# A two-layer decoder trunk: the first norm's modulation in quarters, summed by VectorE and TensorE together, tokens in four loads, rotary angles last

## Chip, cores and metric

One core of one Trainium2 chip. The metric is the device time of one execution in microseconds (us), taken as the median of several runs. A profile is one further execution, recorded by the hardware profiler. Engines: TensorE (PE; PEld is its weight load), VectorE (DVE), ScalarE (ACT), GpSimd (POOL) and SyncE (SP, which here only issues DMAs).

## What is computed

A two-layer causal decoder trunk over 512 tokens of 1024 features, conditioned by a vector c. Each sublayer is a root-mean-square norm with a learned gain, a modulation by c, a mixer or a gated convolutional FFN, a norm, a gate and a residual add. Only the opening matters here: the modulation of the first norm, the normed input h, the values of the first mixer, and the rotary tables that its queries and keys need.

```python
def rms_norm(x, g, eps=1e-6):
    return x * lax.rsqrt(jnp.mean(x * x, axis=-1, keepdims=True) + eps) * g

def ada_mod(c_act, w, b, n):
    return jnp.split((c_act @ w + b)[:, None, :], n, axis=-1)

c_act = jax.nn.silu(c)
ang = positions[..., None] * inv            # rope tables: cos(ang), sin(ang)
shift, scale, gate = ada_mod(c_act, mod_mix_w[0], mod_mix_b[0], 3)
h = rms_norm(x, norm_pre_mix[0]) * (1.0 + scale) + shift
y = dilated_mixer(h, a_w_qkv[0], a_w_o[0], cos, sin)   # 3 groups of 8 heads: q and k rotated, v plain
```

## The kernel before

Each engine has its own program, and semaphores tie them together. A signal such as lo_ready counts the events of a stream; `wait_ge(*at.done(sig, n))` waits for the n-th event from the present count. The order of work on an engine is written out by hand.

**Products.** Values are f32, split into a head (whi, hhi) and a rest (wlo, hlo); a product is three matmuls. Weights come in chunks of 512 KB into raw (three slots). ScalarE makes the head (`split_head`, L1341), VectorE the rest (`split_rest`, L1871, which raises lo_ready), and TensorE waits for lo_ready of the chunk that it multiplies. Chunks 0 to 3 are the values of group 0, chunk 4 is the first of load_pair(0), the first pair of heads.

**The opening, TensorE.** It turns rows of vectors into columns (`turn_rows`, L758; L766 for the rotary constants), then waits for the scaled x (xn0) and turns it, 8 tiles of features by 4 of tokens (L839), into four banks of PSUM, from which ScalarE copies z0 (L1504). Warm-up matmuls (`keep_warm`, L609, 512 columns of bf16, result unused), then `start_sums(0)`: the shift and scale of the first four tiles of features, as 8 sums over partitions of macc0 (L637, each a matmul with one column of f32, two records in the trace). Warm-ups again, then the value products of group 0 (`values_chunk(0, c)`, L800 and L816), 24 matmuls of 512 columns per chunk. Between chunks 0 and 1 stands `shift_columns(4)`: one eighth of the modulation's weights multiplied straight from mstart with csil, 16 matmuls of one column (L781, 32 records). Inside chunk 1 stands start_sums(1), before chunk 2 eight warm-ups. Behind chunk 3 comes first_pair: for each of six chunks a projection of 24 products (L583 to L585), starting with chunk 4.

**The modulation.** csil is silu(c), a column per tile of 128 rows. mod_mix_w for shift and scale is loaded into mstart in eight loads of 1 MB, j = 0 to 7 (L515), rows of 512 columns (2 KB). VectorE multiplies and adds row tiles into macc0 in chains of 8 (`start_chain`, L2162 and L2164: 512 columns each), TensorE sums them over partitions, VectorE adds the bias (`sums_read`, L2183 to L2186) and raises m_known; ScalarE and VectorE then make h: hhi (L1514), tmp (L1513 or L2196), hlo (L2198), which raises h_ready. Work is in halves: four tiles of features at a time.

**x.** SP loads c, five norm vectors, then x in one load of 2 MB (L488), then mstart and the value chunks in turn. ScalarE issues the small loads of its own queue, waits for x, squares four token tiles (L1492), GpSimd takes the root (L2600, L2603) once for the four, ScalarE and VectorE scale two tiles each (L1498, L2151).

**The angles.** VectorE computes them (L2123 to L2133) as soon as the vectors are there, ahead of the scaling and of all sums. ScalarE makes the sine and cosine tables (L1536) before its values_chunk(0, 0). VectorE's last steps of the opening are: split_rest of chunk 3, wait for the sines, the two table products (L2221, L2222), then split_rest of chunks 4, 5 and 6 with halves of the later modulation between them (L2059, L2063), then the rotations (L2233 to L2238). ScalarE's are: the copies of the values (L1521), split_head of chunk 6, the masks (L1548, L1550).

GpSimd makes the masks (L2575) first, then the root, then fetches the later modulations (L2630) once the last load of mstart has landed.

Of the kernel before, what the change touches and what calls it, by code (L numbers as in the profile page):

```python
# [29 lines left out]
P = 128  # L30
# [84 lines left out]
def yoco_trunk(nc, x, c, positions, mod_mix_w, mod_mix_b, mod_ffn_w, mod_ffn_b,  # L115
# [16 lines left out]
    WARM, WARM_START, WARM_SUMS = 12, 8, 12  # L132
# [10 lines left out]
    with ExitStack() as ctx:  # L143
# [234 lines left out]
        x_landed = signal("x_landed", "x_landed", 1, 16)  # L378
# [20 lines left out]
        x_scaled_too = signal("x_scaled_too", "x_scaled_too")  # L399
# [8 lines left out]
        VECS, TABLES, ROWS = 6, 7, 6  # L408
# [55 lines left out]
        def _(sp):  # L464
# [20 lines left out]
            for dst, src in ((PRE_MIX, norm_pre_mix), (POST_MIX, norm_post_mix), (PRE_FFN, norm_pre_ffn), (POST_FFN, norm_post_ffn)):  # L485
                sp.dma_start(rows[dst:dst + 2 * DT, 0, :], src.rearrange("l (r n) -> (l r) n", n=P)).then_inc(*at.here(vec_landed))
            sp.dma_start(rows[KVN:KVN + DT, 0, :], kv_norm.rearrange("(r n) -> r n", n=P)).then_inc(*at.here(vec_landed))
            sp.dma_start(x_tok[:], x[0].rearrange("(t p) d -> p t d", p=P)).then_inc(*at.here(x_landed))  # L488
# [23 lines left out]
            for half in range(2):  # L512
                for j in range(4 * half, 4 * half + 4):
                    col, k0 = half * 4 * P + (D if j % 4 > 1 else 0), j % 2 * (D // 2)
                    sp.dma_start(mstart[:, j], mod_mix_w[0][k0:k0 + D // 2, col:col + 4 * P].rearrange("(k p) n -> p k n", p=P)).then_inc(mods_landed[j].sems[0], 16)  # L515
                for n in (2 * half, 2 * half + 1):
                    load_values(0, n)
# [59 lines left out]
        def _(pe):  # L577
# [9 lines left out]
            def project(rhs, k0, k1, ksteps=DT, first=True, last=True, stride=P, col0=0, done=True, open_=True):  # L587
# [187 lines left out]
            def shift_columns(j):  # L775

                bank = job()
                pe.wait_ge(*at.done(mods_landed[j]))
                for n in range(4):
                    for k in range(DT // 2):  # L780
                        ins = pe.matmul(bank[:, n:n + 1], mstart[:, j, k, tile_cols(n)], csil[:, k:k + 1],  # L781
                                        start=(k == 0), stop=(k == DT // 2 - 1))
                job_done(ins)

            def start_sums(half):

                pe.wait_ge(*at.done(m0_summed, 2 * half + 1))
                columns_of([macc0[:, n, :] for n in range(8)])

            def values_chunk(g, c, between=None):  # L790
# [3 lines left out]
                if g == 0 and c in (0, 2):  # L794
                    for k in (2 * c, 2 * c + 1):
                        pe.wait_ge(*at.done(h_ready, k))
                        w = slice(k % 2 * value_cols(g), (k % 2 + 1) * value_cols(g))
                        for t in range(NT):
                            for n, (a, b) in enumerate(((hhi, whi), (hhi, wlo), (hlo, whi))):
                                mm = pe.matmul(ps[:, t, 0:value_cols(g)], a[:, k, tile_cols(t)], b[:, slot, w], start=(k == 0 and n == 0), stop=False)  # L800
                    mm.then_inc(*at.here(chunk_used))
                    at.passed("chunk")
                    return
                if g == 0:
                    pe.wait_ge(*at.done(h_ready, 2 * c + 1))
                for t in range(NT):
                    if t == 2 and between is not None:
                        between()
                    if g and c == 0:
# [21 lines left out]
            pe.wait_ge(*at.done(x_scaled, 1))  # L831
            pe.wait_ge(*at.done(x_scaled_too, 1))
            for k in range(DT):
                if k < 4:
                    pe.wait_ge(*at.done(t_free, -1 - k % 2))
                else:
                    pe.wait_ge(*at.done(z_out, k - 4))
                for t in range(NT):
                    ins = pe.transpose(ps[:, 4 + k % 4, tile_cols(t)], xn0[:, t, tile_cols(k)], identf[:])  # L839
                ins.then_inc(*at.here(xn_turned, k))  # L840
            pe.wait_ge(*at.done(masks_ready))
            keep_warm(WARM_SUMS, ps[:, 3, :])
            pe.wait_ge(*at.done(z_out, DT - 1))
            start_sums(0)
            keep_warm(WARM_SUMS, ps[:, 3, :])
            values_chunk(0, 0)
            shift_columns(4)
            values_chunk(0, 1, lambda: start_sums(1))
            keep_warm(WARM_START, ps[:, 4, :])
            values_chunk(0, 2)  # L850
            values_chunk(0, 3)
# [471 lines left out]
        def _(act):  # L1323
# [147 lines left out]

            for j, v in enumerate((b_lambda_q1, b_lambda_q2, b_lambda_k1, b_lambda_k2)):
# [1227 lines left out]
```

## Times and profile before

| | us |
|---|---|
| median of 3 runs | 1405.76 (1404.61 to 1405.80) |
| the profiled execution, its own time | 1405.17 |
| its span in the profile | 1403.4 |
| TensorE busy | 1353.8 (96%) |
| VectorE busy | 918.2 (65%) |
| ScalarE busy | 582.2 (41%) |
| GpSimd busy | 147.4 (11%) |
| granted TensorE clock, mean | 0.991 of full |

A busy share is over the whole span. All of the change lies in the first 70 us of it, so the rows below are of that stretch. Times in them count from the span's start.

### The profile page before, as it was taken

To read this page: it belongs to the slowest core of one execution; us is meant where nothing else is said; L and a number is where in the kernel's file an instruction comes from. 1 tells how busy PE (TensorE), PEld (TensorE's weight loads), DVE (VectorE), ACT (ScalarE), POOL (GpSimd) and SP (SyncE) were. 2 spreads that over 40 slices of the span, in tenths; PEclk is the share of its full clock that TensorE was granted. 3 is DMA by queue.
4 is the path that set the end of the run, shared out by engine and by line. 5 is a ranking of instruction groups with operands and counts; after the bars stand their busy time and mean duration, and the time that the engine had idled before them with its cause. 6 is when DMAs were issued, how large, how long until landed. Compare 5 with 4: busy or idle time off the path is not lost.

```text
span 1403.4 us, 17895 instructions
## 1 busy us (share of the span) xinstructions
PE 1353.8 (96%) x6936; PEld 1106.9 (79%) x6936; DVE 918.2 (65%) x1618; ACT 582.2 (41%) x994; POOL 147.4 (11%) x238
## 2 busy tenths in 40 slices
PE   4999999999899999999999999998999999999998
PEld 3789788888788788887887777776888778887886
DVE  7687889886678777764556648997567444443223
ACT  4543344446543334332115537777543333332112
POOL 2001001000411111100113001221220000000000
PEclk9999999999999999999999999999999999999999
DMA  9437424331256555553661232112145333333331
GB/s 332 157 90 221 143 91 151 106 106 46 71 158 207 166 178 181 181 165 101 201 193 65 71 90 61 52 55 91 31 145 161 99 90 91 90 96 99 90 102 64
DMA packets 168665, 171.47 MB, mean 122 GB/s; under 512 B 5269, under 2 KB 140806, under 8 KB 168582
## 3 DMA queue, kind: packets, MB, share of 16 engines
q1 hardware_dynamic: 154224, 119.59, 28.2%
q0 software_dynamic: 13824, 50.34, 10.7%
q8 instruction: 55, 0.90, 0.3%
q10 hardware_dynamic: 534, 0.41, 0.1%
q14 instruction: 28, 0.23, 0.0%
HBM read 168.22 MB, written 2.10 MB: 121 GB/s over the span
## 4 chain that ended last, share of the span: by engine, by line
PE 80%; DVE 9%; ACT 5%; issue 2%; POOL 2%; DMA 1%; SPq 0%; POOLq 0%; ACTq 0%; DVEq 0%
PE ps L655 20%; PE ps L583 15%; PE ps L585 15%; PE ps L584 15%; PE ps L1109 2%; PE ps L816 2%; PE ps L906 2%; ACT prob L1761 2%; PE ps L894 2%; PE ps L626 1%; PE ps L1238 1%; PE ps L637 1%; DVE wlo L1871 1%; DVE prob L2488 1%; POOL osum L2667 1%
## 5 line engine op out<-in xcount | busy, mean ns | idle before, releaser
L583 PE MATMUL ps<-hhi,whi 128*128 128x512 f32 (+1 forms) x1008 | 396.1, 393 | 2.7 <-DVE hlo L1958 2.1
L1871 DVE TENSOR_TENSOR wlo<-raw,whi 128x1024 fp32r<-128x1024 f32 x200 | 244.1, 1221 | 233.8 <-ACT whi L1341 233.7
L585 PE MATMUL ps<-hhi,wlo 128*128 128x512 f32 (+1 forms) x1008 | 387.2, 384 | 0.0
L584 PE MATMUL ps<-hlo,whi 128*128 128x512 f32 (+1 forms) x1008 | 387.1, 384 | 0.0
L1341 ACT ACTIVATE whi<-raw 128x1024 fp32r<-128x1024 f32 x200 | 209.8, 1051 | 244.5 <-PE ps L655 169.5
L583 PEld LDWEIGHTS ps<-hhi,whi 128*128 128x128 f32 x1008 | 189.5, 188 | 45.2 <-DVE hlo L1958 2.9
L585 PEld LDWEIGHTS ps<-hhi,wlo 128*128 128x128 f32 x1008 | 189.4, 188 | 41.4
L584 PEld LDWEIGHTS ps<-hlo,whi 128*128 128x128 f32 x1008 | 189.6, 188 | 39.0 <-issue 1.0
L2063 DVE SCALAR_TENSOR_TENSOR macc<-mraw,csil,macc 128x256 f32<-128x256 f32 x294 | 142.4, 484 | 13.2 <-DMA mraw<-in_mod_ffn_w_dram 4.0
L655 PE MATMUL ps<-whi,ghi 128*128 128x512 f32 x352 | 110.1, 394 | 1.7 <-DVE tmp L2427 1.7
L655 PE MATMUL ps<-whi,glo 128*128 128x512 f32 x352 | 109.1, 391 | 0.0
L655 PE MATMUL ps<-wlo,ghi 128*128 128x512 f32 x352 | 108.9, 390 | 0.0
L2411 DVE SCALAR_TENSOR_TENSOR tmp<-ps,convc,tmp 128x511 f32<-128x511 f32 x88 | 65.9, 748 | 47.8 <-ACT tmp L1699 46.3
L1709 ACT ACTIVATE ghi<-tmp 128x512 fp32r<-128x512 f32 x44 | 27.8, 632 | 154.3 <-DVE tmp L2427 154.3
L1699 ACT ACTIVATE tmp<-ps,convc 128x512 f32<-128x512 f32 x44 | 34.2, 778 | 109.1 <-PE ps L585 109.1
L655 PEld LDWEIGHTS ps<-whi,ghi 128*128 128x128 f32 x352 | 65.7, 188 | 16.8 <-DVE tmp L2427 2.5
L655 PEld LDWEIGHTS ps<-wlo,ghi 128*128 128x128 f32 x352 | 66.1, 188 | 15.1
L655 PEld LDWEIGHTS ps<-whi,glo 128*128 128x128 f32 x352 | 66.1, 188 | 14.1
L2630 POOL DMA_DIRECT2D mraw<-in_mod_ffn_w_dram x48 | 36.4, 759 | 333.3 <-DVE macc L2063 259.3
L2427 DVE TENSOR_TENSOR tmp<-ps,tmp 128x512 f32<-128x512 f32 x44 | 30.4, 690 | 57.3 <-issue 45.0
L2600 POOL TENSOR_SCALAR stat<-stat 128x1 f32<-128x1 f32 (+1 forms) x27 | 14.7, 545 | 431.5 <-ACT tmp L1387 419.0
L1706 ACT ACTIVATE tmp<-tmp 128x512 f32<-128x512 f32 x44 | 27.9, 633 | 52.0 <-DVE tmp L2411 52.0
(306 smaller groups left out, 1961.1 us busy)
## 6 DMA issues: line engine op xcount, KB each, us to landing
mraw<-in_mod_ffn_w_dram POOLq DMA_DIRECT2D x48, 512.0 KB, 4.5
raw<-in_ffn_w_gate_dram SPq DMA_DIRECT2D x44, 512.0 KB, 3.7
raw<-in_ffn_w_up_dram SPq DMA_DIRECT2D x44, 512.0 KB, 3.7
raw<-in_ffn_w_down_dram SPq DMA_DIRECT2D x44, 512.0 KB, 3.6
mraw<-in_mod_mix_w_dram POOLq DMA_DIRECT2D x32, 512.0 KB, 3.9
raw<-in_a_w_qkv_dram SPq DMA_DIRECT2D x28, 512.0 KB, 4.6
mstart<-in_mod_mix_w_dram SPq DMA_DIRECT2D x8, 1024.0 KB, 14.6
mraw<-in_kv_mod_w_dram POOLq DMA_DIRECT2D x16, 512.0 KB, 3.9
```

The costliest lines, as they stand in the source:

```text
L583: pe.matmul(out_, whi[:, slot, cols], rhs_hi, start=first, stop=False)
L584: pe.matmul(out_, whi[:, slot, cols], rhs_lo, start=False, stop=False)
L585: return pe.matmul(out_, wlo[:, slot, cols], rhs_hi, start=False, stop=last)
L655: mm = pe.matmul(ps[:, 2 * t + half, :], part[:, k, tile_cols(t)], w[:, half * 512:half * 512 + 512], start=(first and n == 0), stop=(last ...
L816: mm = pe.matmul(ps[:, t, 0:value_cols(g)], a[:, k, tile_cols(t)], b[:, slot, w], start=(k == 0 and n == 0), stop=(k == DT - 1 and n == 2))
L1341: act.activation(whi[:, slot, :], raw[:, slot, :], ACT.Copy).then_inc(*at.here(hi_ready, ahead))
L1699: act.activation(tmp[:, 0, :], acc[at.at("bank", 3)], ACT.Identity, bias=convc[:, base + 3 * FT + ft:base + 3 * FT + ft + 1], scale=convc[ ...
L1871: dve.tensor_tensor(wlo[:, slot, :], raw[:, slot, :], head, ALU.subtract).then_inc(*at.here(lo_ready, ahead))
L2063: ins = dve.scalar_tensor_tensor(sum_, src, factor, sum_, ALU.mult, ALU.add)
L2411: ins = dve.scalar_tensor_tensor(conv, bank[:, 0:T - shift], tap(t, ft), conv, ALU.mult, ALU.add)
L2427: dve.tensor_tensor(tmp[:, 2, :], bank, tmp[:, 1, :], ALU.mult).then_inc(*at.here(acc_free))
L2630: pool.dma_start(mraw[:, at.at("mod", 2)], src).then_inc(*at.here(m_landed))
```

## The change

- The tokens x are loaded in four loads, a signal each, right behind c on SP's queue; the norm vectors move to ScalarE's queue, the bias and convolution tables to GpSimd's. ScalarE squares a token tile as it lands, GpSimd takes each root by itself, VectorE scales all four.
- The modulation is taken in quarters of two tiles of features: 16 loads of 512 KB, rows of 256 columns (1 KB). Of the eight row tiles of a quarter VectorE adds five in a chain (`chain_sums`), TensorE multiplies the other three straight from mstart (`sums_of`) and adds VectorE's sum into the same columns of PSUM (`close_sums`).
- Value products go a tile of features at a time (`first_values`), with the next quarter's sums between the two tiles of a chunk. The warm-ups have 384 columns (`keep_ready`): 20 ahead of the transposes, 20 ahead of the values, 4 behind each of the first three chunks.
- positions are loaded behind the last quarter of mstart, the angles computed behind the last tile of h, the sines made behind ScalarE's last value chunk. GpSimd's masks come behind its roots.

The diff, cut:

```diff
-    WARM, WARM_START, WARM_SUMS = 12, 8, 12
+    WARM, WARM_FIRST, WARM_QUARTER = 12, 20, 4
...
+        QUARTERS, Z_BANKS = 4, (4, 7, 2, 3, 4, 7, 2, 3)
+        SUMS_V, SUMS_P = ((0, 1, 2), (0, 1)), ((3,), (2, 3))
...
-            sp.dma_start(x_tok[:], x[0].rearrange("(t p) d -> p t d", p=P)).then_inc(*at.here(x_landed))
+            for t in range(NT):
+                sp.dma_start(x_tok[:, t, :], x[0][t * P:(t + 1) * P, :]).then_inc(x_landed.sems[t], 16)
...
+            for q in range(QUARTERS):
+                for j in (2 * q, 2 * q + 1):
+                    rows_of = mod_mix_w[0][j % 2 * (D // 2):(j % 2 + 1) * (D // 2), :]
+                    for part, col in enumerate((2 * q * P, D + 2 * q * P)):
+                        sp.dma_start(mstart[:, j, :, part * 2 * P:(part + 1) * 2 * P],
+                                     rows_of[:, col:col + 2 * P].rearrange("(k p) n -> p k n", p=P)).then_inc(mods_landed[j].sems[0], 16)
+                if q == QUARTERS - 1:
+                    sp.dma_start(posi[:], positions.to_broadcast([P, T])).then_inc(*at.here(pos_landed))
+                load_values(0, q)
...
+            def keep_ready(n, bank):
+
+                for _ in range(n):
+                    pe.matmul(bank[:, 0:3 * P], identb[:], causal[:, 0:3 * P], start=True, stop=True)
...
+            def sums_of(q, half):
+
+                if half == 0:
+                    job()
+                bank = turned[at.at("tjob", 2)]
+                pe.wait_ge(*at.done(mods_landed[2 * q + half], 1))
+                for k in SUMS_P[half]:
+                    for n in range(4):
+                        pe.matmul(bank[:, n:n + 1], mstart[:, 2 * q + half, k, tile_cols(n)], csil[:, 4 * half + k:4 * half + k + 1],
+                                  start=(half == 0 and n == 0 and k == SUMS_P[0][0]), stop=False, skip_group_check=True)
+
+            def close_sums(q):
+
+                bank = turned[at.at("tjob", 2)]
+                pe.wait_ge(*at.done(m0_summed, q))
                 for n in range(4):
+                    ins = pe.matmul(bank[:, n:n + 1], macc0[:, 4 * (q % 2) + n, :], onesf[:, 0:1], start=False, stop=True, skip_group_check=True)
                 job_done(ins)
...
+            def first_values(c):
...
+                for k in (2 * c, 2 * c + 1):
+                    pe.wait_ge(*at.done(h_ready, k))
+                    w = slice(k % 2 * value_cols(0), (k % 2 + 1) * value_cols(0))
+                    for t in range(NT):
+                        for n, (a, b) in enumerate(((hhi, whi), (hhi, wlo), (hlo, whi))):
+                            mm = pe.matmul(ps[:, t, 0:value_cols(0)], a[:, k, tile_cols(t)], b[:, slot, w], start=(k == 0 and n == 0), stop=(k == DT - 1 and n == 2))
...
+                        if c < QUARTERS - 1 and (k % 2, t) == (0, NT - 1):
+                            sums_of(c + 1, 0)
+                            sums_of(c + 1, 1)
+                        if c < QUARTERS - 1 and (k % 2, t) == (1, 0):
+                            close_sums(c + 1)
...
+                else:
+                    keep_ready(WARM_QUARTER, ps[:, 4, :])
...
+            keep_ready(WARM_FIRST, ps[:, 3, :])
+            pe.wait_ge(*at.done(c_ready))
+            pe.wait_ge(*at.done(x_scaled, NT - 1))
...
+            for k in range(4):
+                turn_x0(k)
+            sums_of(0, 0)
+            for k in range(4, DT):
+                turn_x0(k)
+            sums_of(0, 1)
+            close_sums(0)
+            keep_ready(WARM_FIRST, ps[:, 0, :])
+            pe.wait_ge(*at.done(z_out, DT - 1))
+            for c in range(DT // 2):
+                first_values(c)
             pe.wait_ge(*at.done(masks_ready))
...
+            act.preload_act_table(ACT.Exp)
...
+            split_head(0)
             h_head(0, False)
             h_head(1, True)
             split_head(1)
-            h_head(2, True)
+            h_head(2, False)
             h_head(3, True)
             split_head(2)
+            h_head(4, False)
+            h_head(5, True)
+            values_chunk(0, 0)
+            h_head(6, False)
+            h_head(7, True)
+            for c in range(1, DT // 2):
+                values_chunk(0, c)
             act.wait_ge(*at.done(angles_ready))
             for dst, j in ((sinT, 0), (cosT, 1)):
                 act.activation(classed(dst[:]), by_class(ang[:, j, :]), ACT.Sin).then_inc(*at.here(sines_ready))
                 at.passed("sines_ready")
-            values_chunk(0, 0)
-            for k in range(4, DT):
-                h_head(k, False)
-            for c in range(1, DT // 2):
-                values_chunk(0, c)
...
+            scale_tokens(0)
+            scale_tokens(1)
             bank = job_ready()
             job_read(dve.tensor_copy(small[:, NEGLAM:NEGLAM + 1], bank[:, 0:1]))
+            scale_tokens(2)
             for dst, n in ((bcol[:], NMOD), (convc[:, 0:CONV], CONV), (convc[:, CONV:2 * CONV], CONV)):
                 read_columns(dst, n)
+            scale_tokens(3)
...
+            chain_sums(0)
+            sums_read(0)
             split_rest(0)
             h_rest(0, False)
             h_rest(1, True)
+            for q in range(1, QUARTERS):
+                chain_sums(q)
+                if q < QUARTERS - 1:
+                    split_rest(q)
+                else:
+                    at.passed("chunk")
+                    split_rest()
+                sums_read(q)
+                h_rest(2 * q, False)
+                h_rest(2 * q + 1, True)
+            angles()
             at.passed("h", DT)
 
             dve.wait_ge(*at.done(sines_ready, 1))
...
-            pool.wait_ge(*at.done(x_squared, NT - 1))
-            rms(X_RMS, X_SUM, slice(0, NT)).then_inc(*at.here(x_scale))
+            for t in range(NT):
+                pool.wait_ge(*at.done(x_squared, t))
+                rms(X_RMS, X_SUM, slice(t, t + 1)).then_inc(*at.here(x_scale, t))
...
-            pool.wait_ge(*at.done(mods_landed[DT - 1]))
+            pool.wait_ge(*at.done(mods_landed[DT - 1], 1))
```

## Rows read from the trace of the kernel before

**Rows 1.** The chain of waits, 0 to 110 us: start, us, what.
```profile
21.50 6.33 PE ps L839 x32
...
37.68 5.49 PE ps L800 x24
43.17 3.46 PE ps L781 x32
46.63 4.45 PE ps L816 x12
51.09 1.68 PE ps L637 x16
52.77 2.88 PE ps L816 x12
...
62.88 5.49 PE ps L816 x24
```

**Rows 2.** Timeline, VectorE from 40 us: start, us, engine, line, operation.
```profile
59.48 0.48 DVE L2221 TENSOR_SCALAR sinT<-sinT,small 128x512 f32<-128x512 f32 x1
...
60.58 1.23 DVE L1871 TENSOR_TENSOR wlo<-raw,whi 128x1024 fp32r<-128x1024 f32 x1
```

**Rows 3.** Timeline, the start of the opening, 0 to 20 us.
```profile
6.41 0.39 DVE L2095 TENSOR_TENSOR lamr<-lamr 1x128 f32<-1x128 f32 x1 [1.11 <-DMA posi<-in_positions_dram]
...
12.43 1.06 ACT L1492 ACTIVATE tmp<-x_tok 128x1024 f32<-128x1024 f32 x1 [4.27 <-DMA x_tok<-in_x_dram]
...
18.11 1.05 POOL L2603 TENSOR_TENSOR stat<-stat,neghalf 128x4 f32<-128x4 f32 x1
```

**Rows 4.** The page: a group of GpSimd's DMA issues, then issues with us to landing.
```profile
L2630 POOL DMA_DIRECT2D mraw<-in_mod_ffn_w_dram x48 | 36.4, 759 | 333.3 <-DVE macc L2063 259.3
...
mraw<-in_mod_mix_w_dram POOLq DMA_DIRECT2D x32, 512.0 KB, 3.9
...
mstart<-in_mod_mix_w_dram SPq DMA_DIRECT2D x8, 1024.0 KB, 14.6
```

**Rows 5.** Windows: us, busy of five engines, PEclk, DMA share, GB/s.
```profile
20.00:30.00 10.00, 8.50 (x43) 7.24 (x44) 9.61 (x15) 6.74 (x11) 0.00 (x0) 1.00 1.05 387
48.00:49.00 1.00, 1.00 (x4) 0.77 (x3) 1.00 (x2) 0.00 (x0) 0.00 (x0) 0.50 0.00 0
51.00:52.00 1.00, 1.00 (x12) 1.00 (x10) 0.00 (x0) 0.00 (x0) 0.00 (x0) 1.00 1.10 326
```

**Rows 6.** Timeline: the last eight transposes of x, and ScalarE's copies.
```profile
26.68 1.16 PE L839 MATMUL ps<-identf,xn 128*128 128x128 f32 x8
...
26.66 2.05 ACT L1504 ACTIVATE z<-ps 128x512 f32<-128x512 f32 x4
```

**Rows 7.** Timeline: a chain of sums, and the first two tiles of h.
```profile
25.89 5.48 DVE L2164 SCALAR_TENSOR_TENSOR macc<-mstart,csil,macc 128x512 f32<-128x512 f32 x7
...
33.88 0.81 ACT L1514 ACTIVATE hhi<-z,modc,presc 128x512 fp32r<-128x512 f32 x1 [5.17 <-DVE presc L2186]
...
36.14 0.69 DVE L2198 TENSOR_TENSOR hlo<-tmp,hhi 128x512 fp32r<-128x512 f32 x1 [0.65 <-ACT hhi L1514]
```

**Rows 8.** Timeline: the first and the last of VectorE's steps of the angles.
```profile
10.27 0.43 DVE L2123 CAST ang<-posi 128x512 f32<-128x512 int32 x1
...
16.00 0.69 DVE L2133 TENSOR_SCALAR ang<-ang 128x1024 f32<-128x1024 f32 x1
```

**Rows 9.** Timeline, ScalarE: the last copy of values, and the head of chunk 6.
```profile
68.41 0.60 ACT L1521 ACTIVATE vA<-ps 128x512 f32<-128x512 f32 x1 [0.78 <-PE ps L816]
68.91 1.05 ACT L1341 ACTIVATE whi<-raw 128x1024 fp32r<-128x1024 f32 x1
```

**Rows 10.** Timeline, ScalarE: the sine table's load and the two tables.
```profile
40.85 1.28 ACT L1536 ACT_TABLE_LOAD   x1
42.14 1.15 ACT L1536 ACTIVATE sinT<-ang 128x512 f32<-128x512 f32 x1
...
43.20 1.13 ACT L1536 ACTIVATE cosT<-ang 128x512 f32<-128x512 f32 x1
```

More of the change, by code:

```diff
@@ L783, in shift_columns @@
                 job_done(ins)
[L785 to L790, printed above, removed]
+            def first_values(c):
+                slot = at.at("chunk", 3)
+                pe.wait_ge(*at.done(lo_ready))
+                for k in (2 * c, 2 * c + 1):
[4 more added lines that the diff above has]
+                            mm = pe.matmul(ps[:, t, 0:value_cols(0)], a[:, k, tile_cols(t)], b[:, slot, w], start=(k == 0 and n == 0), stop=(k == DT - 1 and n == 2))
+                        if k == DT - 1 and t < NT - 1:
+                            mm.then_inc(*at.here(v_ready))
+                            at.passed("vtok")
+                        if c < QUARTERS - 1 and (k % 2, t) == (0, NT - 1):
[3 more added lines that the diff above has]
+                            close_sums(c + 1)
+                mm.then_inc(*at.here(chunk_used))
+                at.passed("chunk")
+                if c == DT // 2 - 1:
+                    at.passed("vout", NT)
+                else:
+                    keep_ready(WARM_QUARTER, ps[:, 4, :])
@@ L792, in values_chunk @@
+            def values_chunk(g, c):
                 pe.wait_ge(*at.done(lo_ready))
                 slot = at.at("chunk", 3)
[L794 to L803, printed above, removed]
@@ L804, in values_chunk @@
-                if g == 0:
-                    pe.wait_ge(*at.done(h_ready, 2 * c + 1))
                 for t in range(NT):
-                    if t == 2 and between is not None:
-                        between()
-                    if g and c == 0:
+                    if c == 0:
                         pe.wait_ge(*at.done(v_out, t - NT))
@@ L2101, in _ @@
             read_columns(vcol[:], NVEC)
-            read_columns(small[:, 0:5], 5)
             dve.wait_ge(*at.done(c_exped))
@@ L2162, in start_chain, with chain_sums @@
+            def chain_sums(q):
+                sum_ = macc0[:, 4 * (q % 2):4 * (q % 2) + 4, :].rearrange("p a n -> p (a n)")
+                for half in range(2):
+                    dve.wait_ge(*at.done(mods_landed[2 * q + half], 1))
+                    for k in SUMS_V[half]:
+                        src, row = mstart[:, 2 * q + half, k, :], 4 * half + k
+                        if half == 0 and k == 0:
                             ins = dve.tensor_scalar(sum_, src, csil[:, row:row + 1], None, ALU.mult)
@@ L2192, in h_rest @@
                     gain, shift = presc[:, k:k + 1], modc[:, MIX[0] + k:MIX[0] + k + 1]
[L2193 removed]
+                    dve.wait_ge(*at.done(m_known, k // 2))
                     if k >= 3:
@@ L2580, in _ @@
             chain(pool.memset(neghalf[:], -0.5))
+            chain(pool.memset(causal[:], 0.0))
             chain(pool.memset(identf[:], 0.0))
```

189 lines of the change are left out of this document (63 added, 126 removed).

## The prediction

> **What bounds the kernel now.** The chain of waits over the first 110 us [rows 1] says what sets the end of each stage. TensorE is on it nearly throughout and, from 68.4 us on, without a hole; over the span it is 96% busy. So the change, which touches only the code before the projections of the first pair of heads, is worth what it does to one instant: when TensorE can start that pair. Before, that is 68.37 us: the last value product ends there [rows 1], and the next matmul follows at once.
>
> Behind the transposes of x (from 21.50 us) come warm-up matmuls, 8 column sums, warm-ups again, and at 37.68 us the value products. From there to 68.37 us are 30.7 us: 96 products at 22.0 us (24 in 5.49), and 8.7 us of others: the 16 sums of shift_columns (3.46), 12 products at nearly half pace (4.45 instead of 2.75), the 8 sums of start_sums (1.68), and eight warm-ups. Note the counts: 16 sums in the code are x32 in the row, 8 are x16. A sum of one f32 column goes in two passes and costs 3.46/16 = 0.216 us, nearly a product of 512 columns.
>
> The first pair needs weight chunk 4 split by VectorE, and in the code that split stands behind the sine and cosine tables. Before, VectorE makes the tables at 59.48 and splits chunk 4 at 60.58 us, ready at 61.8 [rows 2]: a cover of 6.5 us, because the angles were computed at 10 to 17 us and the sines in the middle of the value products.
>
> **The start.** The five norm loads now stand on ScalarE's queue ahead of five small ones, so the last small one is issued at about 4.3 us instead of 2.4. The last one before was consumed at 6.41 us, 4.0 after its issue [rows 3]; I take 8.0 now. VectorE waits for it before it reads the vectors, so the squares of x start at about 9.3 us instead of 12.43 [rows 3]; x, issued 2.2 us earlier, is no longer the late one. Four squares at a pitch of 1.18 end at 14.1; GpSimd's power took 1.05 for four columns [rows 3], for one column and its addition I take 1.0; VectorE's scaling of the last tile 0.75: 15.9 us. The seven table loads move to GpSimd's queue. A load of 512 KB occupies it 0.76 us [rows 4], so seven end by about 8 us, before its first root at 10.5, and land before VectorE reads them at 14.7: nothing; up to 2 us if they land late.
>
> TensorE does not go straight on: 20 warm-ups of 384 columns stand ahead of its wait for the scaled x, and can't start before the table rows are turned, about 15.4 us. What they cost depends on the clock. The windows give it as 1.00 [rows 5]. But of the 32 transposes, 6.33 us in all [rows 1], the last eight take 1.16 [rows 6], so the 24 before them take 5.2, a pitch of 0.215, half the pace: TensorE was at its lower level (1.2 GHz) for 5.2 us after its idle time. At 0.32 us each until then and 0.17 after, 20 warm-ups cost 5.8 us; at full clock 3.4. The Trainium skill, in "TensorE: Matmul & The Clock Gate", Part 1, says the half-rate state is the default of an idle array; by that rule the trace agrees, in its transposes and not in its recorded clock. By the recorded clock alone all that follows would come 2.4 us earlier; I go by the pace of the transposes. They now start at 21.2 us: nothing gained on 21.50 so far.
>
> They are at full clock then, so ScalarE's copies (a pitch of 0.49 [rows 6]) and the 12 sums between and behind them set the pace: 1.7 for 16 transposes, 0.9 for four sums, 1.7 again, 1.7 for eight sums, 0.9 for the closing four: 7.0. Then 20 warm-ups of 0.17: the value products start 10.4 us after the transposes, at **31.6 us** instead of 37.7. Beside these warm-ups VectorE reads the sums, splits chunk 0 and makes the first two tiles of h.
>
> **The quarters.** TensorE, per quarter: 24 products 5.49, 16 sums 3.46, four warm-ups 0.69: 9.6 us. VectorE: five chained sums instead of eight, 0.5 + 4 x 0.78 = 3.6 (seven took 5.48 [rows 7]), a split 1.1, reading sums 0.5, two tiles of h 2.9 (33.88 to 36.8 [rows 7]): 8.1 us, beside TensorE. So TensorE bounds, and what VectorE gives up is paid by it at 0.216 a sum. Four times 5.49, three times 3.46 and 0.69 are 34.4 us, where there were 30.7. The value products would end at **66.0 us**.
>
> The clock comes on top. 12 sums in a row, three products, 4 sums: that is 3.46 us of sums in 4.15. Behind 3.46 us of sums in a row the windows show 0.50 [rows 5] and 12 products lost 1.7 us; behind 1.68 us of them 12 products took 2.88, hardly more than at full clock [rows 1]. The new stretch is nearer to the first. I take two drops in three quarters, 3.3 us; ends 0 and 6.6 (three, and one ahead of the values). End at **69.3 us**.
>
> Data are in time. The first stage moves 387 GB/s in rows of 2 KB and more; rows of 1 KB are now loaded, and a window with only these shows 326 [rows 5]. At that rate the last quarter lands at about 40 us and is wanted at 51. It turns late below some 240 GB/s.
>
> **The wait that is new.** The angles now stand behind the last tile of h on VectorE, at about 65 us, and the tables and the split of chunk 4 still stand behind them. The angles took 10.27 to 16.69 us, 6.4 us [rows 8]: done at 71. ScalarE first copies out the last values and splits the head of chunk 6, as at 68.41 and 68.91 before [rows 9]: free 1.7 us behind the last product, 71.0; then it loads the sine table (1.28) and makes the two (2.2) [rows 10]: 74.5. VectorE's table products take 1.1, the split of chunk 4 1.2 [rows 2]: ready at 76.9 us. TensorE, which went from values to pair without a pause, now idles 7.6 us behind the last product, whenever that comes. 76.9 - 68.3 = **+8.6 us**.
>
> Then it restarts on the lower level. Time at half pace loses half of itself: 2.6 us by the 5.2 after the idle time at the start, 1.7 by the drop behind the sums. The restart is the nearer row: +2.6. Ends 0 (the clock stays up) and 3.4 (twice the drop).
>
> Behind that nothing is new: VectorE has chunk 5, two mod halves and chunk 6 ahead of the first rotation, 6.2 us of work for a first chunk of 5.6 to 8.2; the masks on ScalarE fit there too. GpSimd's later modulations wait for the last quarter, 40 instead of 37.9 us, and aren't wanted before 65.
>
> **Sum:** start -6.1, longer value stage +3.7, drops +3.3 (0 to 6.6), 7.6 idle, restart +2.6 (0 to 3.4): +11.1 us. The profiled execution took 1405.17 us (span 1403.4), the median of the runs is 1405.76, 0.6 above. So 1416.3 in its terms, and **1416.9** as a median. A measurement of this kernel tells about 0.2%, 2.8 us, from no change.
>
> **Rivals.**
> A, slower, but less: the sums don't drop the clock, since they come in two parts with products between: +7.8, 1413.6.
> B, slower, and more: each quarter drops it, and so do the sums ahead of the values: +14.4, 1420.
> C, not slower: the tables don't hold the split, or come early enough, so that the pair starts behind the last product: without the idle time and its restart, +0.9 with two drops, -2.4 with none, and -4.8 with the opening warm-ups at full clock too: 1401 to 1406.7. It decides where the sines are done before about 64 us. Against: VectorE's text has the angles behind h_ready of the last tile, and before, the split at 60.58 did follow the tables. For: nothing but that the cover was large.
> D, much slower: loads late. Each 1 MB load is now two of 512 KB. Loads of 1 MB landed 14.6 us after issue [rows 4] while the queue moved 387 GB/s, so they overlap. Were the small ones not to, at 3.9 us each (a 512 KB load by itself [rows 4]), the 23 up to the last quarter would end at 90 us where 51 will do: +39 more, 1456. The Trainium skill, "DMA: Bandwidth & Descriptors", Bandwidth, asks for loads of 1 MiB or more; by its fit a load of 512 KB takes an estimated 3.2 us, which one after the other would give nearly the same.
>
> **Chances.** The forecast 0.48, A 0.18, B 0.14, all slower; C 0.11, of it 0.05 faster and 0.06 within 2.8 us; D 0.03, slower; an opening that comes out 3 us earlier, together with A and a cheap restart, 0.06, half of it within. So slower 0.86, same 0.09, faster 0.05. The range leaves out D and most of C: 1408.5 (A with an early opening or a restart at nothing) to 1421.5 (B, tables a little late).
>
> **What would show it.** Right: squares from 9 to 10 us; value products from 30 to 33 us and ending at 65 to 71; sums x24 and x8 a quarter; granted clock 0.50 in places inside the value products; angles on VectorE from 60 to 66; then a hole of TensorE of 7 to 8 us, ended by VectorE's split, and a first pair that starts at half level. Wrong: no such hole, or one under 5 us; sums at half the price; VectorE idle ahead of its sums on a DMA; or a first pair that starts below 72 us.

## The result, and the profile after

| | before | after |
|---|---|---|
| median, us (4 runs each, side by side) | 1405.78 (1404.61 to 1408.53) | 1424.70 (1420.18 to 1429.21) |
| ratio of times, 95% interval | 1 | 1.0135 (1.0114 to 1.0156) |
| profiled execution, its span, us | 1405.17, 1403.4 | 1429.21, 1427.4 |
| granted TensorE clock, mean | 0.991 | 0.983 |

Slower by 18.9 us in medians; 11.1 had been forecast, and the time lies above the range. The profiled execution of after is the slowest of its four: its span is 24.0 us longer. So the accounting below adds up to 24.0, and what was the same in every run is sorted out afterwards.

The chain of waits of after, 0 to 110 us; columns as in [rows 1]. L812 is a value product, L792 the sums straight from mstart, L800 the closing sums, L613 the warm-ups, L864 the transposes.

```profile
4.58 5.47 DMA row<-in_b_subln_dram
...
17.72 6.15 PE ps L613 x20
23.87 1.75 PE ps L864 x16
...
31.09 4.62 PE ps L613 x20
35.71 2.76 PE ps L812 x12
38.47 2.91 PE ps L792 x24
41.38 1.49 PE ps L812 x3
42.87 1.50 PE ps L800 x8
44.37 3.63 PE ps L812 x9
...
51.43 2.57 PE ps L792 x24
...
56.70 4.05 PE ps L812 x9
...
69.05 4.05 PE ps L812 x9
...
74.40 5.71 PE ps L812 x24
80.63 1.05 ACT whi L1368
81.70 1.28 ACT L1561
82.99 1.11 ACT sinT L1561
84.10 1.00 ACT cosT L1561
85.13 0.50 DVE sinT L2233
85.65 0.56 DVE cosT L2234
86.23 1.24 DVE wlo L1891
```

What to see. The value products start at 35.71 us; before, at 37.68 [rows 1]. The last ends at 80.11 (74.40 + 5.71); before, at 68.37. Each of the first three quarters has its sums, x24 and x8, with three products between them (1.49, 1.20 and 0.81 us) and nine behind them in 3.6 to 4.05 us. At full clock, where 24 take 5.49 [rows 1], three take 0.69 and nine 2.06. The last quarter, which has no sums in it, takes 5.71 for its 24. Then TensorE leaves the chain: ScalarE's head of chunk 6, the sine table's load, the two tables, VectorE's two table products and its split of chunk 4, in just the order of the prediction.

Windows of after: the first two while the first sums run, one in the nine products behind them, one in the hole, one in the first pair; columns as in [rows 5].

```profile
39.00:40.00 1.00, 1.00 (x11) 1.00 (x11) 0.21 (x1) 0.00 (x0) 0.11 (x1) 1.00 0.35 130
40.00:41.00 1.00, 1.00 (x9) 1.00 (x9) 0.00 (x0) 0.00 (x0) 1.00 (x2) 0.78 0.60 184
46.00:47.00 1.00, 1.00 (x4) 0.72 (x3) 0.47 (x1) 1.00 (x3) 0.00 (x0) 0.50 0.01 4
85.00:86.00 1.00, 0.00 (x0) 0.00 (x0) 0.84 (x2) 1.00 (x4) 0.00 (x0) 0.50 0.00 0
88.00:89.00 1.00, 1.00 (x3) 0.73 (x3) 0.96 (x3) 0.98 (x3) 0.00 (x0) 0.50 0.19 57
```

By windows of 0.5 us, the granted clock of after was at its lower level (1.2 GHz, 0.50 of full) from 30.3 to 33.7, 40.6 to 47.4, 54.2 to 61.0, 67.9 to 74.7 and 84.9 to 91.8 us: once for 3.4 us, ahead of the values, and four times for 6.8.

Timeline of after: the first and two later products of the first pair, with the idle time ahead of the first in brackets.

```profile
87.60 0.77 PE L587 MATMUL ps<-hhi,whi 128*128 128x512 f32 x1 [7.50 <-DVE wlo L1891]
...
91.58 0.48 PE L587 MATMUL ps<-hhi,whi 128*128 128x512 f32 x1
92.36 0.40 PE L587 MATMUL ps<-hhi,whi 128*128 128x512 f32 x1
```

A record of 0.39 or 0.40 is the full pace here (the step from one product to the next is 0.233 us, a third of 0.70). The first nine of the pair took 3.98 us (87.60 to 91.58) and not 2.10, so the restart cost 1.9 to 2.0.

| part of the 24.0 us | forecast | in this profile |
|---|---|---|
| value products start | -6.1 | -2.0 |
| value stage without a drop, 34.4 for 30.7 | +3.7 | +3.7 |
| drops of the clock in it | +3.3 | +10.0 (44.4 less 34.4) |
| TensorE idle | +7.6 | +7.5 |
| restart | +2.6 | +2.0 |
| later than the first pair | 0 | +2.8 |

The last row is not of the change. A load of the later modulation landed 7.1 us after its issue, the sums waiting for it came 27.4 us behind their reference point and not 25.9, and one stage of 48 products ran at a granted clock of 0.70 to 0.73 in 10.0 us and not 8.4. In the profiles of before and of all the experiments below, the same places showed 25.9 to 26.3 and 8.44 to 8.46. The part behind the start of the first pair differs from profile to profile anyway: 1335.0 us in before, 1339.8 in after, and 1333.2 (3) to 1340.0 (6) in the experiments. Without this row the profile's change is 21.2, and the medians' 18.9 lies 2 us under that; that the number of drops differs from run to run (shown below) would do for such a spread, but no run ties the one to the other.

### The profile page after: what moved, and what is told of

Read it like the earlier page. It is cut to its first block, busy times and chain, and to the rows that moved or that the text cites. A ratio compares the mean times of both kernels' runs of the same rounds, so it can differ in the third digit from the quotient of the medians.

```text
span 1427.4 us, 18078 instructions
## 1 busy us (share of the span) xinstructions
PE 1372.1 (96%) x7018; PEld 1122.1 (79%) x7020; DVE 914.5 (64%) x1616; ACT 580.6 (41%) x993; POOL 156.4 (11%) x251
## 4 chain that ended last, share of the span: by engine, by line
PE 80%; DVE 9%; ACT 5%; issue 2%; POOL 2%; DMA 1%; ACTq 0%; POOLq 0%; DVEq 0%
PE ps L664 19%; PE ps L587 15%; PE ps L589 14%; PE ps L588 14%; PE ps L1136 2%; PE ps L812 2%; PE ps L933 2%; ACT prob L1781 2%; PE ps L921 2%; PE ps L840 2%; PE ps L635 1%; DVE wlo L1891 1%; PE ps L1265 1%; DVE prob L2500 1%; PE ps L613 1%
## 5 line engine op out<-in xcount | busy, mean ns | idle before, releaser
L2439 DVE TENSOR_TENSOR tmp<-ps,tmp 128x512 f32<-128x512 f32 x44 | 30.3, 689 | 57.6 <-issue 45.2
L2607 POOL TENSOR_SCALAR stat<-stat 128x1 f32<-128x1 f32 x30 | 17.0, 566 | 438.8 <-ACT tmp L1414 420.3
```

What stands on the lines that cost most here:

```text
L2439: dve.tensor_tensor(tmp[:, 2, :], bank, tmp[:, 1, :], ALU.mult).then_inc(*at.here(acc_free))
```

## The experiments

Two theories of where the time is lost, and they don't exclude each other: **the tables** (the late angles hold the split of chunk 4, so TensorE idles and restarts low, 9 to 11 us) and **the row of sums** (12 one-column sums in a row let the clock drop, so each of three quarters loses over 3 us). The rival of the second: the sums cost what they cost by their number, or by what VectorE does, and not by their place. Medians of before below are those of the runs beside the experiment. The ratios are taken over all runs of a kernel and are not quite the quotient of the medians. The span of a single profile strays by some us from the medians, so verdicts go by ratios and by the times of the stages.

**1. Angles early.** After, with positions loaded on ScalarE's queue, the angles behind the first chain of sums, the sines behind split_head(2).

```diff
+            act.dma_start(posi[:], positions.to_broadcast([P, T])).then_inc(*at.here(pos_landed))
...
             chain_sums(0)
+            angles()
             sums_read(0)
...
             split_head(2)
+            act.wait_ge(*at.done(angles_ready))
+            for dst, j in ((sinT, 0), (cosT, 1)):
+                act.activation(classed(dst[:]), by_class(ang[:, j, :]), ACT.Sin).then_inc(*at.here(sines_ready))
```

> The changed kernel with the angles computed by VectorE behind its first chain of sums, where it sat idle for 8 us, and the sines made ahead of the fifth tile of h. Theory (the wait for the tables costs 7.5 us of idle TensorE and about 2 us of restart at half level): no hole in front of the first pair, the pair starts 7 to 9 us earlier at full clock, and the time falls by 9 to 11 us, to 1413.5 to 1415.5. Rival 1 (the split of chunk 4 is held by something else, or ScalarE's sines in the middle delay h by as much): a hole of over 4 us stays or moves into the value products, 1420 or more. Rival 2 (the later stage, where sums of the next modulation come late, absorbs it): the pair starts earlier, but the end moves by less than 5 us.

Measured: 1412.78 beside 1404.79, ratio 1.0057 (1.0034 to 1.0079); after itself has 1.0135. Its timeline, the last value product and the first of the pair:

```profile
76.08 0.40 PE L810 MATMUL ps<-whi,hlo 128*128 128x512 f32 x1
76.32 0.39 PE L585 MATMUL ps<-hhi,whi 128*128 128x512 f32 x1
```

No hole and no restart: 0.24 us apart, at full pace. The gain is 0.0078 of 1405, 11 us. The value stage still takes 42.6 us (33.70 to 76.3), with the drops in it (two windows, and from the chain the nine products of the quarter between them):

```profile
40.00:50.00 10.00, 10.00 (x39) 7.79 (x39) 6.85 (x12) 6.62 (x7) 1.62 (x2) 0.67 0.49 159
...
60.00:70.00 10.00, 10.00 (x49) 8.41 (x48) 4.62 (x10) 3.17 (x4) 0.00 (x0) 0.69 0.18 53
```

```profile
53.60 3.76 PE ps L810 x9
```

The sums stand as in after, and yet the three drops were not alike: by windows of 0.5 us the clock was at 0.50 for 6.8, 3.4 and 6.8 us. In the middle quarter it cost 1.7 us (3.76 for 2.06), the price of the drop in before.

**2. Late angles alone.** Before, with the same two moves made in it and nothing else.

```diff
             for c in range(1, DT // 2):
                 values_chunk(0, c)
+            act.wait_ge(*at.done(angles_ready))
+            for dst, j in ((sinT, 0), (cosT, 1)):
+                act.activation(classed(dst[:]), by_class(ang[:, j, :]), ACT.Sin).then_inc(*at.here(sines_ready))
...
             split_rest()
+            a0, a1, k0 = ang[:, 0, :], ang[:, 1, :], ang[:, 2, :]
...
             at.passed("h", DT)
```

> The kernel before, in which only the angles are moved behind the last tile of h and the sines behind the last values; loads, halves and sums stay as they were. Theory: a hole of 7 to 8 us ahead of the first pair and a restart at half level for 3 to 5 us: 8.5 to 10.5 us slower than before, 1414 to 1416.5. Rival (the cover of 6.5 us in the kernel before was real and the hole comes from the quarters): 0 to 2 us slower, 1405.5 to 1408.

Measured: 1416.61 beside 1404.79, ratio 1.0079 (1.0056 to 1.0102). The waits of TensorE (total, times, longest), then the chain:

```profile
PE ps L583 <- DVE wlo L1871: 7.5, 1, 7.5
```

```profile
60.30 5.51 PE ps L816 x24
66.33 1.05 ACT whi L1341
67.39 1.28 ACT L1541
...
71.93 1.24 DVE wlo L1871
```

The same hole of 7.5 us without anything else of the change. The chain shows why it has nothing to do with when the values end: it begins with ScalarE's work behind the last product (66.33) and runs 7 us from there. In this kernel the values end 2.6 us earlier, and the pair gains none of it. Of the 2.6, VectorE's being rid of the angles ahead of the scaling gave 0.9 (the 8 sums start at 30.58 us, not 31.46); the other 1.7 is that the clock did not drop ahead of the values in this profile (the 12 warm-ups there took 2.61 us, in before 4.30). Behind the hole the clock stayed at 0.50 until 78.2 us, so that the restart cost 2.4 us here.

**3. Sums spread.** After, with three sums behind each group of three products, and the closing sums one group later.

```diff
-                        if c < QUARTERS - 1 and (k % 2, t) == (0, NT - 1):
-                            sums_of(c + 1, 0)
-                            sums_of(c + 1, 1)
-                        if c < QUARTERS - 1 and (k % 2, t) == (1, 0):
+                        if c < QUARTERS - 1 and k % 2 == 0:
+                            piece_of(c + 1, t)
+                        if c < QUARTERS - 1 and (k % 2, t) == (1, 1):
                             close_sums(c + 1)
```

> The changed kernel with the same 12 sums per quarter put three behind each group of three products instead of 12 in a row. Theory (it is their crowding that drops the clock): the clock stays at 1.00, the value products take 35 to 37 us, time 7 to 10 us less, 1415 to 1418. Rival (their number sets the price; spread, each also breaks the products' pipeline): value stage of 42 us or more and 1423 to 1426, clock at 0.50 in the products or not.

Measured: 1415.40 beside 1404.79, ratio 1.0078 (1.0052 to 1.0105). A window of the value stage, then from the timeline the first of the pair:

```profile
40.00:50.00 10.00, 9.91 (x61) 8.18 (x60) 6.86 (x12) 3.18 (x4) 1.07 (x2) 1.00 0.44 144
```

```profile
76.40 0.77 PE L587 MATMUL ps<-hhi,whi 128*128 128x512 f32 x1 [7.51 <-DVE wlo L1901]
```

As many sums as in after, but the clock is at 1.00 throughout the values and the stage takes 35.9 us (33.0 to 68.9), not 44.4. The place of the sums was the cost, not their number. The hole stays at 7.51.

**4. VectorE takes all eight rows.** After, with only the four closing sums left on TensorE (three rows fewer for it, three more for VectorE).

```diff
-        SUMS_V, SUMS_P = ((0, 1, 2), (0, 1)), ((3,), (2, 3))
+        SUMS_V = ((0, 1, 2, 3), (0, 1, 2, 3))
...
-                            sums_of(c + 1, 0)
-                            sums_of(c + 1, 1)
```

> The changed kernel with all eight row tiles of a quarter summed by VectorE; TensorE only closes (4 sums a quarter instead of 16). Theory (TensorE's 12 one-column sums cost 2.6 us a quarter and drop its clock for 6.8 us each time): the granted clock stays at 1.00 through the value products, VectorE bounds with 10.5 us a quarter, the value products take 37 to 39 us instead of 44.4, and the stage ahead of them is 2 us shorter: 8 to 10 us less, 1415 to 1417. Rival (VectorE's three extra steps per quarter, 2.3 us, take back what TensorE gains; the drops come from the closing sums or the waits): value stage of 43 us or more, 1421 to 1425.

Measured: 1416.35 beside 1404.79, ratio 1.0077 (1.0052 to 1.0101). The waits of TensorE, the chain, a window:

```profile
PE ps L789 <- DVE macc L2172: 6.1, 3, 2.8
```

```profile
58.34 1.41 PE ps L789 x8
59.75 4.05 PE ps L801 x9
```

```profile
60.00:70.00 10.00, 10.00 (x34) 7.40 (x34) 8.10 (x16) 5.24 (x7) 0.00 (x0) 0.72 0.19 55
```

The value stage takes 40.2 us, because TensorE now waits 6.1 us for VectorE's sums. The time came out as expected (1415 to 1417), but neither the clock (1.00 throughout) nor the stage (37 to 39 us) did: behind four closing sums that had waited up to 2.8 us the clock dropped in all three quarters, twice for 3.4 us and once for 6.8, where nine products took 4.05 us again. So a row of 12 sums is one way to a drop, and a wait with a short row of sums behind it looks to be another; the two parts of that were not tried apart.

**5. Two rows of six.** As 3, but six sums behind the second group of the tile and six behind the fourth, closing behind the sixth group.

```diff
-                for half, k, n in pieces[3 * i:3 * i + 3]:
+                for half, k, n in pieces[6 * i:6 * i + 6]:
...
-                        if c < QUARTERS - 1 and k % 2 == 0:
-                            piece_of(c + 1, t)
+                        if c < QUARTERS - 1 and k % 2 == 0 and t % 2:
+                            piece_of(c + 1, t // 2)
```

> The changed kernel with the 12 sums of a quarter in two rows of six, behind the second and the fourth group of three products, the closing four behind the sixth group. It asks how crowded sums may stand. Theory (a row nearer to the 1.68 us of the kernel before, which kept the clock, does no harm; a row here is 1.3): clock at 1.00 in all three quarters, value stage 35 to 36.5 us, time as a_sums_spread, 7 to 10 us under the changed kernel. Rival (any row of sums beside another loses the clock in part of the quarters): value stage 38 to 42 us, 1418 to 1422.

Measured: 1416.47 beside 1406.62, ratio 1.0072 (1.0048 to 1.0097). A window of its value stage:

```profile
43.00:53.00 10.00, 9.92 (x60) 8.32 (x60) 6.80 (x12) 3.07 (x5) 0.00 (x0) 1.00 0.35 111
```

Clock 1.00 and a stage of 35.8 us. Rows of six sums (1.23 us in the chain) did no harm here with six products between them; rows of 2.6 to 2.9 us did in after.

**6. Closing sums late.** After with its row of 12, the closing four moved two groups of products back. The theory was that a drop lasted 6.8 us because a second row follows close on the first.

```diff
-                        if c < QUARTERS - 1 and (k % 2, t) == (1, 0):
+                        if c < QUARTERS - 1 and (k % 2, t) == (1, 2):
```

> The changed kernel with the row of 12 sums as it is, and only the closing four sums two groups of products later. It asks why each drop lasted about 6.8 us and not 3.3 as in the kernel before. Theory (the closing sums fall into the time at half level and keep it there): the clock still drops behind each row, but for 3.3 to 3.5 us; value stage 38.5 to 41 us instead of 44.4, of which up to 1 us is waiting for h, which now comes later. Rival (the row alone sets the length): three drops of 6.5 us or more, value stage of 44 us or more.

Measured: 1425.73 beside 1406.62, ratio 1.0132 (1.0106 to 1.0158): nothing gained on after. Three windows of its value stage:

```profile
39.00:49.00 10.00, 10.00 (x36) 7.75 (x35) 4.28 (x10) 3.17 (x4) 1.62 (x2) 0.66 0.54 172
49.00:59.00 10.00, 9.22 (x59) 7.66 (x58) 5.64 (x11) 3.18 (x4) 0.00 (x0) 1.00 0.19 54
59.00:69.00 10.00, 10.00 (x51) 8.33 (x50) 5.20 (x10) 1.40 (x2) 0.00 (x0) 0.73 0.18 52
```

The theory falls: the two drops (39.8 to 46.6 and 63.7 to 70.5 us) are still 6.8 us long. And the middle quarter, the same code, did not drop. So whether a row of 2.6 us drops the clock is not settled by the code alone.

**7. Both repairs.** 1 and 3 together.

> Both repairs together in the changed kernel: angles in VectorE's idle time and sines early, sums of TensorE spread three by three. Theory (table wait and clock drops are separate losses that add up): no hole, clock at 1.00 from the value products on, the pair starts at 68 to 70 us as in the kernel before (68.2), time within 2 us of the kernel before, ratio 0.999 to 1.0015. Rival 1 (they overlap, one was hidden in the other): 5 us or more above before. Rival 2 (the quarters gain by themselves once both are gone): 4 us or more below before.

Measured: 1405.34 beside 1406.86 (12 runs and 34), ratio 0.9995 (0.9981 to 1.0009). A window, and from the timeline the end of the values:

```profile
45.00:55.00 10.00, 9.91 (x61) 8.18 (x61) 6.72 (x13) 6.51 (x7) 0.00 (x0) 1.00 0.22 66
```

```profile
69.13 0.40 PE L821 MATMUL ps<-whi,hlo 128*128 128x512 f32 x1
69.37 0.39 PE L585 MATMUL ps<-hhi,whi 128*128 128x512 f32 x1
```

From 1.0135 to 0.9995 is 19.7 us; the repairs one by one gave 11.0 and 8.0. The two causes add up, and what is left of the change is worth nothing that can be told: values 33.61 to 69.37, so 4.1 us earlier at the start and 5.1 longer.

**8. No opening warm-ups.** 7 without the 20 ahead of the transposes.

```diff
-            keep_ready(WARM_FIRST, ps[:, 3, :])
             pe.wait_ge(*at.done(c_ready))
             pe.wait_ge(*at.done(x_scaled, NT - 1))
```

> c_early_spread without the 20 warm-ups ahead of the transposes. Theory (they run at half level for 5 to 6 us while the scaled x is ready some 4 us earlier; they delay more than they warm): transposes start at 18.5 to 19 instead of 22.8, the first 20 or so at the lower level, value products 1 to 3 us earlier, time 1 to 3 us less than c_early_spread. Rival (the time is merely paid later, since transposes and sums then run at the lower level): value products start at the same 33.5 us within 0.7, no difference in time.

Measured: 1407.72 beside 1406.86, ratio 0.9994 (0.9980 to 1.0008). The chain:

```profile
18.96 3.65 PE ps L871 x16
...
29.94 4.95 PE ps L611 x20
```

The transposes start earlier, but at half pace (16 in 3.65 us, where after took 1.75), and the second warm-ups take 4.95 and not 3.27. Values at 34.89, later than in 7. The rival held: the time at the lower level is paid in one place or the other.

**9. Vectors first.** 8, with VectorE reading the vectors before it waits for the last small load, and ScalarE squaring the first token tile before the exponential that this load feeds.

```diff
-            dve.wait_ge(*at.done(row_landed, ROWS - 1))
-            chain(dve.tensor_tensor(lamr[0:1, 0:2, :], lamr[0:1, 0:2, :], lamr[0:1, 2:4, :], ALU.mult))
...
+            dve.wait_ge(*at.done(row_landed, ROWS - 1))
+            chain(dve.tensor_tensor(lamr[0:1, 0:2, :], lamr[0:1, 0:2, :], lamr[0:1, 2:4, :], ALU.mult))
             dve.wait_ge(*at.done(lam_exped))
```

> c_no_opening with VectorE reading the vectors before it waits for the small rotary and lambda loads (10.1 us), and ScalarE squaring x before the exponential of the lambdas. Theory (that small load held the squares of x: predicted at 9.3, they started at 11.1): squares start at 9.0 to 9.6 us, all behind them 1.3 to 2 us earlier, time 1.3 to 2 us less than c_no_opening and below the kernel before. Rival (x or the tables on GpSimd's queue land late next): the transposes start less than 0.7 us earlier.

Measured: 1406.59 beside 1406.86, ratio 0.9992 (0.9975 to 1.0008). The chain holds the reason:

```profile
2.59 6.25 DMA rows<-in_kv_norm_dram
```

The vectors' own last load takes 6.25 us and is there at 8.84 us, where the small one waited for in 8 was there at 9.72 (4.54 + 5.18): 0.9 us gained. So the squares start at 9.73 and not 10.72, the values 0.84 us earlier (34.05). No difference that can be told.

**10. Spread sums in before.** Before, the 16 sums of shift_columns two by two between the products of chunk 0.

```diff
                                 mm = pe.matmul(ps[:, t, 0:value_cols(g)], a[:, k, tile_cols(t)], b[:, slot, w], start=(k == 0 and n == 0), stop=False)
+                            if c == 0:
+                                shift_piece(4, k % 2 * NT + t)
...
-            shift_columns(4)
```

> The kernel before, in which the 16 sums of shift_columns stand two by two between the products of value chunk 0 instead of in a row behind it. Theory (a row of one-column sums drops the clock, spread ones do not): the 12 products behind it take 2.8 instead of 4.45 us, clock at 1.00 there, 1.7 us less than before (ratio 0.9988). Rival: the drop comes anyway, or spreading costs the products as much; no difference, 0.9997 to 1.0005.

Measured: 1405.36 beside 1406.86, ratio 0.9982 (0.9967 to 0.9996). The chain and a window:

```profile
47.98 2.87 PE ps L830 x12
```

```profile
39.00:49.00 10.00, 10.00 (x61) 8.78 (x60) 9.64 (x15) 7.62 (x9) 0.30 (x1) 1.00 0.50 158
```

The 12 products that took 4.45 [rows 1] take 2.87. (The profile's span, 1404.4 us, doesn't show it: in that run the clock was at 0.50 from 31.1 to 37.9 us, the eight sums ahead of the values took 3.54 us, in before 1.92, and the values started at 38.93, not 37.68.) That is 1.6 us by the rows; the ratio gives 2.5, with an interval from 0.6 to 4.6. This is the only kernel of the study whose interval lies under 1, and as one of eleven with an interval that ends at 0.9996 it is a small gain and no firm size.

**11. Fewer warm-ups in 10.** Six instead of 12 ahead of the values.

```diff
-            keep_warm(WARM_SUMS, ps[:, 3, :])
+            keep_warm(WARM_SUMS // 2, ps[:, 3, :])
```

> b_sums_spread with 6 instead of 12 warm-ups between the first column sums and the value products, where the clock is at half level and they take 4.3 us while the first tiles of h are ready after 2 to 3. Theory (they delay): value products start 1 to 2 us earlier, time 0.5 to 1.5 us under b_sums_spread, about 0.997 of the kernel before. Rival (they carry the clock back up, and fewer leave the first products at half level): no difference or up to 1.5 us slower.

Measured: 1404.77 beside 1406.62, ratio 0.9987 (0.9968 to 1.0005). By the times it is not to be told from 10, nor from before. Two windows of the profiled execution, at 1409.96 us the slowest of the twelve:

```profile
34.00:44.00 10.00, 9.50 (x32) 7.52 (x29) 8.52 (x13) 9.97 (x12) 1.80 (x2) 0.50 0.98 336
44.00:54.00 10.00, 10.00 (x33) 8.56 (x33) 5.05 (x7) 1.12 (x2) 0.00 (x0) 0.50 0.20 57
```

The values start at 35.36 us, 2.3 earlier than in before, but the clock was at 0.50 from 33.8 to 54.3 us, all through chunk 0 with its spread sums: that chunk took 17.2 us (35.36 to 52.56), in 10 it took 9.1 (38.93 to 47.98), and the first pair starts at 73.4 us instead of 68.4. It came back only in the 12 products behind, which have no sums between them. So sums in twos did not start a drop in 10, but in 11 a drop that had begun ahead of them did not end while they ran. That is one profile, and the other eleven runs were faster; the rival, that the warm-ups bring the clock back up, fits it.

## Why the prediction went wrong, step by step

The sign and the mechanism came out as forecast, the size did not: +18.9 for +11.1.

- **What bounds it now, and the instant that counts.** Right. The change acts through when the first pair can start: with that instant put back to 69.37 us (68.37 before), the whole loss was gone (7).
- **The drops: the step that failed.** "I take two drops in three quarters, 3.3 us; ends 0 and 6.6." The direction was right (the row of 12 lets the clock fall, 3), but in the profiled run all three quarters dropped, and each drop lost 3.3 us, not 1.65. The 1.65 came from the one drop in before, where the 12 slow products [rows 1] were followed by another row of sums and then by products at nearly full pace: by windows of 0.5 us its clock was at 0.50 for 3.4 us, in each quarter of after for 6.8. Twice as long and once more often make 10.0 for 3.3. Which length a drop has is not fixed by the code: 1, with the sums of after, had both, and so had 4. Rival B, each quarter dropping, had the count right, at 1.65 each; three at 3.3 in the forecast's sum would have given 1423.6. One example of a drop was not a price per drop, and its upper end should have been a multiple of it. The profile's change is 12.9 us more than forecast; this term is 6.7 of them, the start, mis-sized too, 4.1. The median is off by 7.8.
- **The start.** -6.1 forecast, -2.0 in the profile of after, -4.1 and -4.5 in two of the experiments that share this opening (values at 33.61 in 7, 33.22 in 5). Of the 4.1 us missing, 2.3 are ahead of the opening warm-ups (17.72 for 15.4, mostly because the last small load landed at 10.05 and not 8.0), 0.4 in them (6.15 for 5.8), 0.2 in the turning and sums, and 1.2 in the second warm-ups (4.62 for 3.4): the clock fell there too (30.3 to 33.7 us), which I had left to rival B. That is not fixed either: in 1, 3, 5, 6 and 7, with the same 12 and 4 sums ahead of the values, it stayed at 1.00 there and the warm-ups took 3.27. The trace of before had a case of it, in its chain, where 12 warm-ups ahead of the values take 4.30 us and eight of the same kind later 1.74:

```profile
33.38 4.30 PE ps L609 x12
...
55.64 1.74 PE ps L609 x8
```

The placing of the transposes at half pace before and full pace now was right.
- **The sums and the stage.** Right. Sums at the price worked out (24 records in 2.57, that is 12 sums at 0.214; forecast 0.216), and 34.4 us for the stage at full clock: 3 and 5, which have no drops, took 35.9 and 35.8, their sums being split up.
- **The new wait.** Right in kind, place and size: 7.5 us for 7.6, ended by VectorE's split of chunk 4, behind ScalarE's two tables. Experiment 2 shows it alone, 1 shows its end. VectorE's angles ran from 72.4 to 78.8 us and not from 65 to 71, with the values as late, and did not bound it: ScalarE came to the tables only at 81.7.
- **The restart.** 2.0 for 2.6; 2.4 in 2.
- **Loads.** Right: the last quarter had landed by about 40 us and VectorE waited for none of its loads. The 1 us windows from 16 to 38 us gave 347 to 377 GB/s. (The window of 326 that the prediction took for rows of 1 KB moved 637 packets of 512 bytes, of the first pair's weights; it erred on the careful side.) By the Trainium skill, "DMA: Bandwidth & Descriptors", Bandwidth, loads of 1 MiB or more are asked for; no cost of halving them shows here, and rival D is out.
- **Rival C**, not slower, was out by the order of the text, as said. What it named as the deciding point, sines done before about 64 us, is what experiment 1 brought about.
- **The signs.** Of those named as right, the hole, its end, the sums, the 0.50 inside the values and the pair's start at half level came true; the squares (11.05 us for 9 to 10), the start and the end of the values (35.71 and 80.11) and the angles came later than named.

**What stays open:** why a drop lasts 3.4 us in before, 3.4 or 6.8 in 1 and 4, 6.8 in each quarter of after and 20.5 in 11; why one quarter of three did not drop in 6; and with that, whether the 9 us between the runs of after are the number and length of drops. Each kernel has one profile.

## What to carry to other kernels

When a reorder makes an engine finish a long job late, look for what stands behind it in the text of its neighbour: 6.4 us of angles were free while they ran ahead of the sums, and cost 7.5 us of idle TensorE and 2 of restart when their tables stood ahead of a split. One-column matmuls are dear twice, in their own time and in the clock behind them: put products between them. Here rows of 2.6 to 2.9 us came with drops in all quarters but one, while sums in twos, threes or sixes between products (10, 3, 5) started none. They are no way out of one: in 11, entered at the lower level, a chunk with sums in twos stayed there to its end. A stall priced from one example should have a range of several times that example.

## What the runs showed that was not expected

- **A drop outlasts its cause.** In after the granted clock fell late in a row of sums of 2.6 to 2.9 us, or up to 0.9 us behind it (at 40.6, 54.2 and 67.9 us, with rows that began at 38.47, 51.43 and 64.37), and stayed at 0.50 for 6.8 us, through sums and products alike.
- **The recorded clock and the pace disagree in the opening.** The windows of after give a granted clock of 1.00 from 18 to 24 us, yet the 20 warm-ups there took 6.15 us, where in 7 the second 20 took 3.27. The prediction went by the pace and not by the recorded clock, and that held.
- **Small loads were slow while the large queue was full.** A load of one row (row<-in_b_subln, 0.5 KB) took 5.47 us, the vectors' last in experiment 9 6.25 us; before, the last small one was consumed 4.0 us after its issue [rows 3]. That was two of the four us missing from the start. That the large loads in SP's queue are the reason is likely, but no run tried small loads without them.
